# Moving the split weights to another place within a 512-byte stretch of the on-chip memory than the activations they are multiplied with

## What is computed

```python
def swiglu(u, w1, w2):
    gate, up = jnp.split(u @ w1, 2, axis=-1)
    return (jax.nn.silu(gate) * up) @ w2

for i in range(DEPTH):                       # first block
    h = h + 0.5 * rms_norm(swiglu(rms_norm(h, g[0]), ffn_w1[i, 0], ffn_w2[i, 0]), g[1])
    ...                                      # a mixer: convolution + state space, or attention
    h = h + 0.5 * rms_norm(swiglu(rms_norm(h, g[4]), ffn_w1[i, 1], ffn_w2[i, 1]), g[5])

for layer in range(DEPTH):                   # second block
    proj = jnp.einsum('bsd,dc->bsc', h, w_in[layer])     # three mixers and their gates
    ...
    if layer % 2 == 0:
        ff = swiglu_2(h, ffn_w_gate[j], ffn_w_up[j], ffn_w_down[j])
    else:
        ff = moe_swiglu(...)                 # 8 experts, top 2, width 3584
    h = layer_norm_2((DN_ALPHA * h + ff).astype(h.dtype), ...)
```

## Time and profile before

| | us |
|---|---|
| median of 2 runs | 3258.02 (3257.91 to 3258.14) |
| profiled execution | 3260.16 |
| its span, first to last instruction | 3258.4 |
| TensorE busy | 3196.7 (98%) |
| VectorE busy | 2257.7 (69%) |
| ScalarE busy | 1862.8 (57%) |
| DMA | 718.89 MB, mean 221 GB/s |
| mean granted clock of TensorE | 0.995 |

### The profile page before, as it was taken

The page is one execution under the profiler, slowest core; times in us unless marked ns, Lnnn a source line. Parts: engine busy times, 40 slices in busy tenths (PEclk is TensorE's granted clock), DMA queues, the critical chain, the costliest instruction groups (busy, mean ns, idle before and its releaser), DMA issues.

```text
span 3258.4 us, 40388 instructions
## 1 busy us (share of the span) xinstructions
PE 3196.7 (98%) x16131; PEld 2653.7 (81%) x16131; DVE 2257.7 (69%) x2676; ACT 1862.8 (57%) x2461; POOL 24.7 (1%) x44
## 2 busy tenths in 40 slices
PE   9999999999999999999999999999999999999998
PEld 7888588887988878888788887887888888888886
DVE  5559865655446565656655657567899898998998
ACT  5442354544545445646444456564777777777775
POOL 1000000000000000000000000000000000000000
PEclk9999999999999999999999999999999999999999
DMA  9453264664527344534564444336999999999994
GB/s 320 140 175 129 90 228 154 207 200 148 155 78 251 133 173 162 181 130 155 169 207 167 165 160 155 138 122 227 354 364 354 361 356 352 361 355 359 357 353 181
DMA packets 379769, 718.89 MB, mean 221 GB/s; under 512 B 12659, under 2 KB 152321, under 8 KB 379472
## 3 DMA queue, kind: packets, MB, share of 16 engines
q1 hardware_dynamic: 376432, 705.87, 61.1%
q0 software_dynamic: 3056, 10.62, 0.9%
q10 hardware_dynamic: 112, 0.05, 0.0%
HBM read 715.44 MB, written 1.05 MB: 220 GB/s over the span
## 4 chain that ended last, share of the span: by engine, by line
PE 88%; DVE 7%; ACT 3%; issue 1%; DVEq 0%; DMA 0%; SPq 0%; ACTq 0%
PE duo L1038 14%; PE duo L1040 14%; PE duo L1039 14%; PE acc L1038 8%; PE acc L1040 8%; PE acc L1039 8%; PE aux L1038 2%; PE aux L1039 2%; PE aux L1040 2%; PE duo L551 1%; PE duo L550 1%; PE duo L552 1%; PE aux L550 1%; PE aux L551 1%; PE aux L552 1%
## 5 line engine op out<-in xcount | busy, mean ns | idle before, releaser
L1638 DVE TENSOR_TENSOR weights_split<-w,weights_split 128x1024 fp32r<-128x1024 f32 x672 | 790.7, 1221 | 95.8 <-ACT weights_split L1617 94.3
L1617 ACT ACTIVATE weights_split<-w 128x1024 fp32r<-128x1024 f32 x672 | 675.2, 1053 | 242.8 <-PE duo L1040 162.6
L1038 PE MATMUL duo<-weights_split,u_high 128*128 128x512 f32 x1776 | 698.2, 393 | 1.7 <-DVE weights_split L1638 1.7
L1040 PE MATMUL duo<-weights_split,u_low 128*128 128x512 f32 x1776 | 692.6, 390 | 0.0
L1039 PE MATMUL duo<-weights_split,u_high 128*128 128x512 f32 x1776 | 691.8, 390 | 0.0
L424 DVE TENSOR_TENSOR w_low<-w,w_high 128x1024 fp32r<-128x1024 f32 x304 | 368.2, 1224 | 301.2 <-ACT w_high L415 300.0
L1160 DVE TENSOR_TENSOR weights_split<-w,weights_split 128x1024 fp32r<-128x1024 f32 x320 | 377.3, 1222 | 267.2 <-ACT weights_split L1148 267.0
L415 ACT ACTIVATE w_high<-w 128x1024 fp32r<-128x1024 f32 x304 | 318.4, 1057 | 326.0 <-PE aux L1040 88.2
L1148 ACT ACTIVATE weights_split<-w 128x1024 fp32r<-128x1024 f32 x320 | 320.8, 1054 | 238.6 <-PE duo L1040 139.7
L1038 PEld LDWEIGHTS duo<-weights_split,u_high 128*128 128x128 f32 x1776 | 333.9, 188 | 71.0 <-issue 3.3
L1040 PEld LDWEIGHTS duo<-weights_split,u_low 128*128 128x128 f32 x1776 | 333.6, 188 | 70.7
(11 more groups left out here) (431 smaller groups left out, 5060.9 us busy)
## 6 DMA issues: line engine op xcount, KB each, us to landing
w<-in_ffn_w_dram SPq DMA_DIRECT2D x130, 1024.0 KB, 7.7
w<-in_moe_w_gate_dram SPq DMA_DIRECT2D x112, 1024.0 KB, 7.3
w<-in_moe_w_up_dram SPq DMA_DIRECT2D x112, 1024.0 KB, 6.7
w<-in_moe_w_down_dram SPq DMA_DIRECT2D x112, 1024.0 KB, 8.2
w<-in_w_in_dram SPq DMA_DIRECT2D x92, 1024.0 KB, 7.3
w<-in_hyb_w_in_dram SPq DMA_DIRECT2D x18, 1024.0 KB, 8.2
w<-in_ffn_w_gate_dram SPq DMA_DIRECT2D x11, 1024.0 KB, 7.6
w<-in_ffn_w_up_dram SPq DMA_DIRECT2D x11, 1024.0 KB, 10.0
```

The source lines that it names most:

```text
L1038: pe.matmul(bank_out, x_hi, w_hi, start=first, stop=False, skip_group_check=True)
L1040: return pe.matmul(bank_out, x_lo, w_hi, start=False, stop=last, skip_group_check=True)
L1617: act.activation(units[:, place, 0, cut], src[:, cut], ACT.Copy).then_inc(sem("moe_high"), 1)
L1638: m = dve.tensor_tensor(units[:, place, 1, cut], src[:, cut], units[:, place, 0, cut], ALU.subtract)
```

## The change

The two gaps `lead` and `gap` go. The constants `con`, the small scratch `small` and the parameters `par` move from the end to between `w2_high` and `h`. A gap of 32 words (128 bytes) stands ahead of `weights_split`, and one of 96 words (384 bytes) behind it, ahead of `hidden_T_odd`; the arena is 128 words longer, which is these two gaps. No instruction is added, removed or reordered.

```diff
         w_low = sb("w1_low", [P, RING, 4096], F32R)
-        sb("lead", [P, 16])
         with nc.sbuf_tensor("w2", [P, RING2, 2, D], F32) as w2:
             pass
         w_high = sb("w2_high", [P, PIECES, 1024], F32R)
-        sb("gap", [P, 16])
+        con = sb("con", [P, cat["pair16"][0]])
+        small = sb("small", [P, 400])
+        par = sb("par", [P, STACK_ROWS])
         h = sb("h", [P, NT, D])
         u = sb("u", [P, KC, T])
         rows = sb("rows", [P, 2, D])
-        ARENA = 21760
+        ARENA = 21888
...
         uh = sb("u_high", [P, KC, T], F32R)
+        sb("gap_units", [P, 32])
         units = sb("weights_split", [P, 3, 2, 2048], F32R)
+        sb("gap_hidden", [P, 96])
         hT_odd = sb("hidden_T_odd", [P, 2, 2, T], F32R)
-        mGT = sb("arena_rest", [P, ARENA - 21504], F32R)
-        con = sb("con", [P, cat["pair16"][0]])
-        par = sb("par", [P, STACK_ROWS])
-        small = sb("small", [P, 400])
+        mGT = sb("arena_rest", [P, ARENA - 21632], F32R)
```

## The result

| | before | after |
|---|---|---|
| median of 2 runs, us | 3258.02 | 3310.98 (3310.38 to 3311.57) |
| profiled execution, us | 3260.16 | 3311.57 |
| its span, us | 3258.4 | 3309.8 |

The ratio is 1.0158, 95% interval 1.0138 to 1.0179: the change costs 53 us, 1.6%, where 51 us of gain had been predicted. It lies 49 us beyond the range given, and 10 us beyond the upper end of rival C.

A forecast was written before the change was run, and what follows sets the result against it. TensorE, busy 98% and hardly waiting, was taken as bound by the steps between its matmuls. Terms -37.6 - 18.8 - 0.5 + 6.2 = -50.7 us gave 3207 us; own range 3175 to 3240, 8-in-10 range 3148 to 3262.

The forecast's parts named there:

- rival C: Only the distance's size counts, 0 being best: units go from 226.7 to 229 or 231.3 ns, 3276 to 3301 us; chance 0.14.
- What bounds the kernel, and what the change can touch: TensorE, busy 98% of the span, hardly waits; the step between its matmul starts is all the change can touch.
- rival B: The place modulo 512 isn't what matters: steps stay at 227 and 230 ns, 3250 to 3262 us; chance 0.18.
- Part 1: Units moved from difference 0 to +128 bytes: 7992 matmuls fall from 226.7 to 222 ns, -37.6 us.
- The point at -96: Streamed pieces at -64 and -128 bytes, taken as -96 on average at 230 ns, against units at 0 with 226.7.
- The upper bound of part 1: Units' step at +128 is bounded above by what 0 and the worst place cost, 226.7 to 231.3 ns.
- Part 2: Streamed pieces from -64/-128 to +128: 2352 matmuls fall from 230 to 222 ns, -18.8 us; 192 of 256 columns gain 0.5.
- Part 3: Pieces loaded, 256 columns, from +64/+128 to -128: 2400 matmuls rise from 115.7 to 118.3 ns, +6.2 us.
- Parts 4 to 6: Transposes and float32 matmuls, VectorE and ScalarE, the longer arena and the constants between: 0 each.
- The collision with DMA and VectorE: In the experts faster matmuls ask DMA for 364 GB/s: not binding at 222 ns; at the floor 15 us lost.
- Rival A: Conflict vanishes: units and streamed pieces reach the floor, saving 118 us less offsets, 3146 to 3165 us; chance 0.34.
- The floor of 216 ns: Least step of 512 columns once, from float32 matmuls going through the array twice at 430 ns; units pay 10.7 ns over it.

The follow-up runs named there:

- e3: Changed kernel with 128 bytes ahead of the first buffer, so every place moves and every difference stays: 3310.26 us (kernel before 3257.66).
- e13: The stretches: kernel before, with 41 stretches of equal float32r matmuls added behind TensorE's last one, each at a fixed operand distance: 3500.11 us in all.

## Why the prediction was wrong

- *What bounds the kernel, and what the change can touch.* Right. All 51 us are in the distance between the starts of matmuls; TensorE's idle time fell from 50.5 to 48.0 us.
- *The step depends on the difference of the two places, not on each by itself.* Right (e3, and the stretches moved together), and rival B falls, as the changed differences moved every kind of step. But B's first argument, the 2.5 ns between two stretches of pieces with equal places, was sound: the two levels are that "something else" (229 and 231 ns both occur in blocks past `u` and in blocks past the mixers' outputs), and they lie 2 ns apart where the units lost 5.9. At the same difference of +128, units and streamed pieces agree after the change, 233.2 and 232.6.
- *Part 1, the units at 222 ns.* This is the step that failed, and nearly all of the error: 7992 x (233.2 - 222) = 90 us, of the 104 between prediction and result. Its sentence was "the further the streamed operand lies ahead of the loaded one, the cheaper", drawn through two points, carried on by 128 bytes. The runs show that there is no such slope: 0 is a minimum that comes again at 256, 64 costs 229 ns, and nearly all other places tried cost the same 233.
- *Where the slope came from.* The point at -96 "on average" was not a place but a mix, high parts at -64 and low parts at -128. In that stretch -64 alone costs 233.3 and 128 alone 232.3 or 233.3, the mix 231.2. Thus the worst place appeared milder than it is, and the rival C was priced with it (229 to 231.3). The range ended at 3262, the upper end of B, because C, with 0.14, was left out of it. And the order at 256 columns was taken as a second witness for the sign, when it too compared two mixes, and 256 columns have an order of their own.
- *The upper bound of part 1* ("what 0 and the worst place cost, 226.7 to 231.3") took the worst row for the worst place. The changed step was outside both bounds.
- *Part 2, the streamed pieces, -18.8 us.* They got -0.1: +1.1 past `u`, where +128 costs 2 ns more than the mix, and -1.2 past the mixers' outputs. Here a second error: all 2352 were taken at +128, but the outputs lie in the space of `weights_split`, at the very place of the pieces, so that 800 stand at 0 and not at +128. The 192 of 256 columns got +0.2 instead of -0.5.
- *Part 3, the loaded pieces, +6.2 us.* Right in direction and nearly in size, +8.6, but by luck: its reason was the sign, and at 256 columns too +128 and -128 are one place (120.0 in the stretches at 128 and at 384). What was lost is the mix of +64 and +128, which is cheaper than either.
- *Parts 4 to 6.* Near the predicted zero: the other matmuls take 3.6 us less (why was not looked into), VectorE's subtraction 1221 ns at equal places as at different ones, the longer arena nothing.
- *The collision with DMA and VectorE* was never tried, as TensorE became slower.
- *Rival C* had the outcome, and half of the mechanism: 0 was the best place and could only be lost, and -128 costs what +128 costs. Its words "only the size counts" are wrong (+64 costs 229 ns, -64 233, and 256 as little as 0). It was given 0.14 and 229 to 231.3 ns a unit; 233.2 is 3310 by its own sum. Its argument was the right one: a row at 512 columns spoke for it, and only rows at 256 columns, six steps of them, against.
- *Rival A*, a conflict that goes away altogether, doesn't occur in any layout tried: no stretch of 512 columns is below 226.6 ns, whatever the difference. Its upper end, by its own terms, is 3161 and not 3165.
- *The floor of 216 ns* was taken from the float32 matmuls, so that these "pay nothing" is not a finding but how the floor was set. The 430 ns are the step from one record to the next, and a single float32 matmul of e13 leaves two such records, so "twice" holds of a record at most. Whether a float32r matmul can reach 216 no run shows.

The prediction quoted the Trainium skill, "SBUF — State Buffer", Who interferes with whom, for two independent read ports of TensorE. The stretches disagree: with every other engine idle, the same matmul takes 226.7 or 233.6 ns by where its two operands lie to each other.

**What stays open.** Why 0 and 64 are cheap at 512 columns and 192 at 256; what sets the level of a block; why -64 mixed with -128 is cheaper than both when 0 mixed with -64 is just their mean; and what the 10.7 ns are that even the best place pays over the earlier trace rows. No run here had a float32r matmul without a load beside it, which would tell whether those 10.7 ns belong to the load.

## What to carry to other kernels

Where TensorE never waits, look at the distance between the starts of its matmuls by operand pair, and give float32r operands of 512 streamed columns the same place modulo 256 bytes: 6 ns of 233 were at stake in each, against 1 to 2 between the two levels at one difference. Measure the few candidate places in a stretch of equal matmuls, at the number of columns that the kernel streams, before buffers are moved, and expect the kernel to differ from it by a level; a mixed triple is not a measurement of a place. And don't carry on a line through two points of a quantity that depends on an address: expect it to be periodic, and ask first whether the present place is already the minimum.

## What the runs showed of the hardware

- A float32r matmul with a load of 128 columns beside it: 226.7 ns (512 columns), 202.7 (448), 173.3 (384), 119.6 (256) at difference 0; at the clock of 2.4 GHz, which was granted in full in these stretches, 226.7 ns are 544 cycles, 32 more than columns.
- The dearer places add 12 to 24 cycles to that, most of them 16 (560, 233.3 ns); 64 bytes add 5. At 256 columns the best place, 192, has 272 cycles, 16 more than columns.
- At one and the same difference a long block holds one of two steps: 232.3 or 233.3 ns (512 columns, +128), 113.4 or 117.8 (256 columns, -64), 118.7 or 120.0 (256 columns, -128).
- The period is 256 bytes, and differences below 32 bytes count too: 4 bytes gave the longest step of all, 236.6 ns.
- The Trainium skill, "TensorE: Matmul & The Clock Gate", Wait — 56ns, not 53.3ns?, gives 215.7 ns for successive starts of 512 columns at full clock. No stretch of float32r matmuls with a load beside each came down to it: 226.6 ns is the least. The float32 ones, with 430 ns from record to record, have twice the page's figure.
